# Which engine computes the rests of the rounded weights: from GpSimd to fixed places in the vector engine's order

## What is computed

```python
xn = rms_norm(x, norm_w)
z  = xn @ w_in                                     # 2048 columns in, 8384 out
y_r, S_T = rwkv7_branch(mix(zs), g_r, S0, ...)     # recurrence, gated
o_att    = sum over 3 patterns of dilated_band_attention(q, k, v, ...) * silu(g_a)
y = x + concatenate([y_r, o_att]) @ w_out
```

## Time and profile before

| | |
|---|---|
| median of the 3 runs shown | 1743.68 us (1742.6 to 1744.62) |
| span of the profiled execution, first to last instruction | 1741.7 us |
| what lies around the span, against that median | 2.0 us |
| TensorE busy | 1626.1 us, 93% |
| vector engine (DVE) busy | 814.8 us, 47% |
| ScalarE (ACT) busy | 571.7 us, 33% |
| GpSimd (POOL) busy | 529.7 us, 30% |
| of that the rests, L426, x164 | 397.8 us |

### The profile page before, as it was taken

One profiled execution on the slowest core, in us unless ns is written; L12 is line 12 of the kernel. 1 busy time (PEld: TensorE's weight loads), 2 busy tenths in 40 slices (PEclk: granted clock), 3 DMA queues, 4 the chain that ended last, 5 costly groups with the idle time before them and its releaser, 6 DMA issues.

```text
span 1741.7 us, 32851 instructions
## 1 busy us (share of the span) xinstructions
PE 1626.1 (93%) x12525; PEld 1491.2 (86%) x12525; DVE 814.8 (47%) x1326; ACT 571.7 (33%) x935; POOL 529.7 (30%) x256
## 2 busy tenths in 40 slices
PE   5999989999899998999989999999999999789998
PEld 4988979889798897988979988898888988569998
DVE  3145564655646557465575544263443634420000
ACT  5242232422324223232242333334343343432221
POOL 0333232232322323223142223232232332433432
PEclk9999999999999999999999999999999999899999
DMA  5320220302203022030220544435344363525443
GB/s 185 93 73 18 63 58 3 105 13 62 58 1 103 17 63 58 1 96 25 56 73 26 131 104 121 88 99 139 78 121 98 89 139 78 153 73 146 127 113 87
DMA packets 249819, 140.88 MB, mean 81 GB/s; under 512 B 11053, under 2 KB 242798, under 8 KB 249198
## 3 DMA queue, kind: packets, MB, share of 16 engines
q1 hardware_dynamic: 228156, 126.23, 28.2%
q10 hardware_dynamic: 21570, 13.23, 2.5%
HBM read 124.11 MB, written 15.26 MB: 80 GB/s over the span
## 4 chain that ended last, share of the span: by engine, by line
PE 84%; DVE 7%; issue 4%; ACT 1%; DMA 1%; SPq 1%; POOL 1%; DVEq 0%; ACTq 0%; POOLq 0%
PE acc L442 50%; PE head_banks L858 5%; PE head_banks L882 5%; PE head_banks L1035 2%; PE head_banks L1062 2%; PE head_banks L1017 2%; PE head_banks L894 2%; DVE AREN L1523 2%; PE head_banks L1029 1%; DVE AREN L1585 1%; PE head_banks L792 1%; PE head_banks L759 1%; DVE AREN L1763 1%; PE head_banks L775 1%; PE head_banks L910 1%
## 5 line engine op out<-in xcount | busy, mean ns | idle before, releaser
L426 POOL TENSOR_TENSOR WL<-WR,WH 128x1024 fp32r<-128x1024 f32 (+1 forms) x164 | 397.8, 2426 | 943.4 <-ACT WH L418 935.2
L442 PE MATMUL acc<-XH,WH 128*128 128x260 f32 (+1 forms) x2624 | 595.6, 308 | 20.1 <-POOL XL L692 10.3
L442 PE MATMUL acc<-XL,WH 128*128 128x260 f32 (+1 forms) x2624 | 531.6, 284 | 0.0
L442 PE MATMUL acc<-XH,WL 128*128 128x260 f32 (+1 forms) x2624 | 531.5, 284 | 0.0
L442 PEld LDWEIGHTS acc<-XH,WH 128*128 128x128 f32 (+1 forms) x2624 | 412.0, 191 | 59.6 <-issue 29.3
L442 PEld LDWEIGHTS acc<-XL,WH 128*128 128x128 f32 (+1 forms) x2624 | 408.2, 190 | 0.0
L442 PEld LDWEIGHTS acc<-XH,WL 128*128 128x128 f32 (+1 forms) x2624 | 407.5, 190 | 0.0
L418 ACT ACTIVATE WH<-WR 128x1024 fp32r<-128x1024 f32 (+1 forms) x164 | 171.7, 1047 | 147.0 <-PE acc L442 123.9
L652 POOL TENSOR_TENSOR AREN<-AREN,CA 128x1024 f32<-128x1024 f32 x40 | 87.0, 2176 | 163.6 <-PE head_banks L858 81.3
L1226 ACT ACTIVATE AREN<-head_banks 128x512 f32<-128x512 f32 x80 | 47.9, 599 | 215.2 <-PE head_banks L894 114.1
L858 PE MATMUL head_banks<-AREN 128*128 128x128 f32 x640 | 89.4, 299 | 22.0 <-DVE AREN L1585 19.3
(11 more groups left out here) (234 smaller groups left out, 1939.1 us busy)
## 6 DMA issues: line engine op xcount, KB each, us to landing
WR<-in_w_in SPq DMA_DIRECT2D x128, 512.0 KB, 4.1
WR<-in_w_out SPq DMA_DIRECT2D x32, 512.0 KB, 5.8
out<-AREN ACTq DMA_DIRECT2D x32, 256.0 KB, 2.7
AREN<-in_cache_k_win SPq DMA_DIRECT2D x16, 384.0 KB, 8.5
AREN<-in_cache_v_win SPq DMA_DIRECT2D x16, 384.0 KB, 8.6
mix_scratch<-AREN ACTq DMA_DIRECT2D x16, 260.0 KB, 2.6
AREN<-in_x_prompt SPq DMA_DIRECT2D x4, 1024.0 KB, 7.9
AREN<-in_cache_k_win SPq DMA_DIRECT2D x8, 512.0 KB, 7.3
```

Source lines behind the costliest of these rows:

```text
L426: pool.tensor_tensor(WL[:, k % 2, :, 0:M], WR[:, k % 4, :, 0:M], WH[:, k % 2, :, 0:M].bitcast(F32), ALU.subtract).then_inc(s_lo, 1)
L442: mm = pe.matmul(acc[0:M, hf, 0:HT], w[:, k % 2, j, 0:M], x[:, kt, hf * HT:(hf + 1) * HT], start=(kt == 0 and n == 0), stop=(kt == KT - 1 ...
```

## The change

GpSimd keeps the gate, the five masked products and the slope products; the rests that it formed in the pairs (8 in each of the 8 recurrence pairs, 8 in each of the first 7 attention pairs) go to the vector engine, each at one fixed place of its order. GpSimd still forms those ahead of the first pair and those of the output projection, and the vector engine waits once for the former, GpSimd once for the last of the moved ones.

```diff
-        def rest_half(pool, g, k, M=128):
+        def rest_half(eng, g, k, M=128):
...
-        def pool_feed(pool, span, g, name, ahead=True):
-            for u in span[name]:
-                if u % 8 == 1 and (ahead or u // 8 < 7):
-                    rest_half(pool, g, u // 8 + 1)
...
-                for name in ("lora", "kk", "tail", "bonus", "vec", *GRAMS):
-                    feed(name)
...
-                    if l == 1:
-                        for name in ("tokb", "tokk", "tokv", "nn23", "bcast"):
-                            feed(name)
-                    if l > 1:
-                        for s in ("qt", "dx", "tr"):
-                            for h in "ab":
-                                feed(f"{s}{l - 1}{h}")
-                for name in PE_A.names[PE_A.index[f"qt{last - 1}a"]:]:
-                    feed(name)
...
+            pool.wait_ge(s_lo, 4 * GROUP_C + 1)
             rest_half(pool, GROUP_C, 1)
...
+            dve.wait_ge(s_lo, 4 * group_a(0) + 9)
+
+            def pair_a(i, g, next_shift=True):
...
                    .then_inc(a_dve, DVE_A.one("ssm"))
+                rest_half(dve, g, 1)
...
                    .then_inc(a_dve, DVE_A.one("prod"))
+                rest_half(dve, g, 2)
...
                     for h in range(2):
                         masked(c, h, banks[h])
+                    if c == 2:
+                        rest_half(dve, g, 3)
...
                         dve.tensor_copy(flat(QT[:, 4:8, :]), HB[:, 0, :]).then_inc(a_dve, DVE_A.one(f"qt{l}"))
...
+                    if l in (1, 5):
+                        rest_half(dve, g, 4 + l // 5)
                     for h in range(2):
                         dve.wait_ge(a_pe, PE_A.at(i, f"dx{l}{'ab'[h]}"))
...
                 after("sw")
+                rest_half(dve, g, 6)
                 state(1)
...
                 state(2)
+                rest_half(dve, g, 7)
...
                     shift(i + 1, group_a(i + 1))
+                rest_half(dve, g, 8)
...
                 qs.then_inc(b_dve, DVE_B.one("qs"))
+                rest(1)
...
                 dve.tensor_tensor(GGB, GGB, ZB[:, 3, :], ALU.mult).then_inc(b_dve, DVE_B.one("gate"))
+                rest(2)
...
+                    if t == 1:
+                        rest(3)
...
+                    if j in (0, 2, 5):
+                        rest({0: 4, 2: 5, 5: 6}[j])
                     if j + 2 < nj:
                         largest(j + 2)
...
                    .then_inc(b_dve, DVE_B.one("smx"))
+                rest(7)
...
                 dve.tensor_tensor(MIXB[:, 0:T], HB[:, 3, :], GGB[:, 0:T], ALU.mult).then_inc(b_dve, DVE_B.one("mixp"))
+                rest(8)
```

More of the change, by code:

```diff
@@ L418, in round_half @@
             act.activation(WH[:, k % 2, :, 0:M], WR[:, k % 4, :, 0:M], ACT.Copy).then_inc(s_hi, 1)
-        def rest_half(pool, g, k, M=128):
-            pool.wait_ge(s_w[k % 4], (g + (k // 4 + 1)) * 16)
-            pool.wait_ge(s_hi, g * 4 + (k + 1))
+        def rest_half(eng, g, k, M=128):
+            eng.wait_ge(s_w[k % 4], (g + (k // 4 + 1)) * 16)
+            eng.wait_ge(s_hi, g * 4 + (k + 1))
             if not (isinstance(g, int) and 4 * g + k < 2):
-                pool.wait_ge(s_half, g * 4 + (k - 1))
-            pool.tensor_tensor(WL[:, k % 2, :, 0:M], WR[:, k % 4, :, 0:M],
+                eng.wait_ge(s_half, g * 4 + (k - 1))
+            eng.tensor_tensor(WL[:, k % 2, :, 0:M], WR[:, k % 4, :, 0:M],
                                WH[:, k % 2, :, 0:M].bitcast(F32), ALU.subtract).then_inc(s_lo, 1)
@@ L636, in _, with pair_a @@
                 rest_half(pool, group_a(0), k)
-            def pair_a(i, g, ahead=True):
-                def feed(name):
-                    pool_feed(pool, span_a, g, name, ahead)
+            def pair_a(i):
                 pool.wait_ge(a_act, ACT_A.at(i, "sgg"))
                 pool.tensor_tensor(GG, GG, Z[:, 3, 1:TT + 1], ALU.mult).then_inc(a_pool, POOL_A.one("gate"))
-                for name in ("lora", "kk", "tail", "bonus", "vec", *GRAMS):
-                    feed(name)
                 for l in range(1, last):
@@ L653, in pair_a, with pair_b @@
                         .then_inc(a_pool, POOL_A.one(f"nm{l}"))
-                    if l == 1:
-                        for name in ("tokb", "tokk", "tokv", "nn23", "bcast"):
-                            feed(name)
-                    if l > 1:
-                        for s in ("qt", "dx", "tr"):
-                            for h in "ab":
-                                feed(f"{s}{l - 1}{h}")
-                for name in PE_A.names[PE_A.index[f"qt{last - 1}a"]:]:
-                    feed(name)
[L664 to L673, removed]
+            with pool.Fori(0, PAIRS) as i:
+                pair_a(i)
+            def pair_b(i):
                 pool.wait_ge(b_dve, DVE_B.at(i, "sl"))
@@ L681, in pair_b @@
                     .then_inc(b_pool, POOL_B.one("bts"))
[L682 to L687, removed]
+            with pool.Fori(0, PAIRS) as i:
+                pair_b(i)
+            pool.wait_ge(s_lo, 4 * GROUP_C + 1)
             rest_half(pool, GROUP_C, 1)
@@ L1508, in shift @@
                 mix.then_inc(a_mix, DVE_M.one("mix"))
-            def pair_a(i, next_shift=True):
+            dve.wait_ge(s_lo, 4 * group_a(0) + 9)
+            def pair_a(i, g, next_shift=True):
                 def after(name):
@@ L1676, in _ @@
             with dve.Fori(0, PAIRS - 1) as i:
-                pair_a(i)
-            pair_a(PAIRS - 1, next_shift=False)
+                pair_a(i, group_a(i + 1))
+            pair_a(PAIRS - 1, group_b(0), next_shift=False)
             dve.wait_ge(a_pe, PE_A.start(PAIRS))
@@ L1690, in _, with pair_b, rest @@
             dve.wait_ge(s_zero, 2)
-            def pair_b(i):
+            def pair_b(i, g, fills=True):
+                def rest(k):
+                    if fills:
+                        rest_half(dve, g, k)
                 def after(name):
@@ L1792, in pair_b @@
                 ms.then_inc(b_dve, DVE_B.one("mixs"))
-            with dve.Fori(0, PAIRS) as i:
-                pair_b(i)
+            with dve.Fori(0, PAIRS - 1) as i:
+                pair_b(i, group_b(i + 1))
+            pair_b(PAIRS - 1, 0, fills=False)
             dve.wait_ge(o_mix, done(PAIRS, PAIRS, 16))
```

## The result

The changed kernel takes 1747.17 us (median of 15 runs, 1743.21 to 1751.4), the kernel before 1743.64 us beside it (15 runs, 1740.55 to 1746.15). The ratio is 1.002, with a 95% interval of 1.0012 to 1.0028: slower by 0.2%, 3.5 us. The forecast was 1750.0 us, its own range 1744 to 1756.

A forecast was written before the change was run, and what follows sets the result against it. TensorE, busy 1626.1 of 1741.7 us, was taken as the bound, so only its waits count. Recurrence +8.7 and attention -2.3, about +6.3 us with rounding, on 1743.7 gave 1750.0 us, own range 1744 to 1756, 8 in 10: 1737 to 1765.

The forecast's parts named there:

- wait before `bonus`: Recurrence, L775: scans no longer held by GpSimd's rest 1, so `prod` comes earlier; six pairs -1.0, two -0.4: -6.8 us.
- spells of 1.2 GHz: Recurrence, behind L775: the wait falls to 1.7 us and draws no slow-clock spell; 5 x -1.55 = -7.7 us.
- rest 2: Recurrence, behind `prod`: waits for its rounding but loses a block, ending just before TensorE reaches the grams; cost nothing, cover 0.1 us.
- rest 3, before L780: Recurrence: partly hidden in a 0.70 us idle hole, the remainder reaches TensorE through the fourth chunk's grams; 8 x 0.4 = +3.2 us.
- wait before the first level: Recurrence, L858: `nm2` holds `xtm` or `xt` instead of a rest, `xtb` comes 0.3 us earlier; -2.4 us, spells left there.
- rest 4 behind `nm3`: Recurrence, between `qt1` copy and `xa`: held by GpSimd, it makes TensorE's L894 2.0 us late; +16.0 us, the largest term.
- rest 5: Recurrence, level 5: no `nm` beside it, a 0.2 us gap hides part; some +0.8 us each, +6.4 us.
- `pn`: Attention, first block: no longer slowed beside a GpSimd rest, so TensorE's 0.7 us wait per pair goes; 7 x -0.7 = -4.9 us.
- rest 7, before `pwt`: Attention, behind `smx`: `spm` starts 0.5 us later, 0.3 us of TensorE's time taken; 7 x 0.3 = +2.1 us.
- The faster one: Rival, recurrence: the slightly shorter wait before L858 draws no slow-clock spell; 9 x -1.56 = -14 us, 1736 us; chance 0.20.
- the slower one: Rival, recurrence: the new 2.0 us wait before L894 draws a spell in every pair; +12.5 us, 1762.5 us; chance 0.20.
- rest 4 gets ahead of `nm3`: No-change rival, recurrence: or it is not held by `nm3`, costing 0.8 us; 9.6 us go, 1740.4 us; chance 0.13.

The follow-up runs named there:

- all places: Changed kernel with rests 4 and 5 behind `xb`, `nm2` behind `xtb`, scans to `gl` ahead of `ssm`, rest 3 behind the last masked gram: 1684.39 us, ratio 0.9659.
- two changed orders: Kernel before, all rests on GpSimd, scans to `gl` ahead of `ssm`, rest 4 and `nm2` behind it held until `xtb`: 1692.14 us, ratio 0.9701.
- the one with the scans first: Kernel before, all rests on GpSimd, with the scans and decay steps to `gl` moved ahead of `ssm` on the vector engine: 1718.96 us, ratio 0.986.

## Why the prediction was right

The direction, the mechanism and most terms held; the sum was +6.3 us and +3.4 came out, by the two spans. Term by term, measured from the two profiles:

| term | forecast | measured | from |
|---|---|---|---|
| wait before `bonus` | -6.8 | -4.5 | 18.2 and 1.4 of waits for a rest just before it in pairs 0 and 7, to 15.1 |
| spells of 1.2 GHz | -7.7 | -10.9 | 15 to 8, at 1.55 us |
| rest 2 | 0 | 0 | from L775 to the matmuls of L792 that wait, and from L748 to those of L765, 10.71 us without a spell |
| rest 3, before L780 | +3.2 | +2.7 | 2.0 to 4.7 |
| wait before the first level | -2.4 | -1.7 | 22.0 to 20.3, with pair 7 |
| rest 4 behind `nm3` | +16.0 | +16.7 | below |
| rest 5 | +6.4 | +6.1 | below |
| the loop's edge | none | -1.1 | 10.3 to 9.2 |
| **recurrence** | **+8.7** | **+7.3** | the stretch itself: +7.2 |
| `pn` | -4.9 | -5.5 | 0.92 in each of pairs 1 to 6, below |
| rest 7, before `pwt` | +2.1 | +1.6 | 0.24 in each of pairs 1 to 6, 0.15 in pair 0, start to start |
| late load, pair 0 | +0.5 | +0.2 | the wait 3.99 to 4.52; the step behind it 0.19 later |
| **attention** | **-2.3** | **-3.7** | the stretch itself: -3.8 |

**Rests 4 and 5.** The wait that the profile shows for rest 4, 1.80 us, is less than what it costs. Where nothing is waited for, the transposes (L894) begin 0.15 us before the matmuls ahead of them (L882) end, by the ends that the profile gives, and this overlap is lost too. The cost is read from start to start, in pairs without a spell, first the kernel before (pair 7):

```profile
911.82 2.02 PE L858 MATMUL head_banks<-AREN 128*128 128x128 f32 x16 [2.72 <-issue]
913.68 2.10 PE L882 MATMUL head_banks<-AREN 128*128 128x128 f32 x16
915.63 0.61 PE L894 MATMUL head_banks<-CA,AREN 128*128 128x128 f32 x4
...
917.97 1.95 PE L858 MATMUL head_banks<-AREN 128*128 128x128 f32 x16
```

and the kernel after (pair 4):

```profile
587.13 2.05 PE L831 MATMUL head_banks<-AREN 128*128 128x128 f32 x16 [2.53 <-DVE AREN L1562]
...
595.37 1.95 PE L831 MATMUL head_banks<-AREN 128*128 128x128 f32 x16
```

One level took 6.15 us and takes 8.24, 2.09 more: the forecast was 2.0. Pairs 0 to 2, with a spell in this level in both kernels, give 1.82 to 2.14. The level of rest 5, read in the same way, went from 6.18 to 6.94 us: 0.76, where 0.8 was forecast. The rest itself took 2.52 us and ended 1.08 us after `nm3`, as worked out. The Trainium skill (SBUF — State Buffer, "Who interferes with whom") has the engine that issues first hold the port for its whole instruction, and the row of 2.52 us, behind an `nm3` that began 0.56 us earlier, agrees.

**The attention.** There, too, more goes than the profile's wait. In the attention's pair 2 the step from the first L1017 to the first L1035 (L990 and L1008 after), first before, then after:

```profile
1150.15 0.38 PE L1017 MATMUL head_banks<-AREN 128*128 128x128 f32 x2
...
1156.15 0.43 PE L1035 MATMUL head_banks<-AREN 128*64 128x128 f32 x2
```

```profile
1156.87 0.38 PE L990 MATMUL head_banks<-AREN 128*128 128x128 f32 x2
...
1161.95 0.43 PE L1008 MATMUL head_banks<-AREN 128*64 128x128 f32 x2
```

It went from 6.00 to 5.08 us: 0.92, where the wait for `pn` had been 0.71. The whole pair went from 72.00 to 71.32 us, and each of pairs 1 to 6 did the same within 0.03.

**What was mis-sized.** "6 x -1.0 and 2 x -0.4" for rest 1: only five pairs had the wait of 2.67 us in the trace of before. Pair 6 stood at 1.51 already, and pairs 0 and 7 gained nothing, because a wait for GpSimd's rest of 0.7 us just ahead of `bonus` went into the longer wait at `bonus` itself. That is 2.3 us too much gain. In the other direction, "I leave the spells there" for the wait before the first level: two of its seven spells went, and two double ones became single ones, and the one behind the loop's edge went, against two new ones behind L867 and one behind L748. The count came to -7, not -5, and the gain to 3.2 us more. In the attention "7 x -0.7" had one pair too many, since pair 0 had no such wait, and too little for each, 0.92.

**The rivals.** The faster one (the seven spells behind the first level go) came true in two pairs of seven, the slower one (a new spell behind L894 in each pair) in two of eight: each is a matter of degree. That the sum came near is in part luck: the prediction left the spells behind the first level as they were, and its 2.3 us too much gain at rest 1 and 3.2 too little at the spells nearly cancelled. That rest 4 gets ahead of `nm3` did not happen. The Trainium skill's rule (Perfetto Trace Analysis, "Optimizing Scalar/DVE Operations") that moving work between these two engines might not help fits this change as it stands, 1747.2 us. With all places the move gives 1684.4, and two changed orders with no rest moved give 1692.1: the places decide, and the move is worth some 8 us on top of them.

## What to carry to other kernels

When work moves between the vector engine and GpSimd, look first at which instruction comes next behind the new place, and which GpSimd instruction is released by the same event; the costliest place here was between the copy and the subtraction that TensorE waits for. Try the order before the move: here two changed places in the kernel before gain 3.0%, and the move on top of that 0.4%. Read a new wait from start to start of the same step, since the idle time shown for it was 1.80 us where 2.09 were lost.

## What the runs showed of the hardware

**A one-operand instruction is held too.** The prediction spoke of vector instructions with two operands in SBUF, though its `pn`, 2.29 us beside a rest, is a `TENSOR_SCALAR` with one tensor operand. `t1`, which reads one tensor from SBUF, took 492 ns in the median in the kernel before and 2528 in the one with the scans first, beside GpSimd's rest. Those with an operand in PSUM, `xa` and `xb`, kept 0.69 us beside `nm2` and `nm3`.

**The length of a wait alone does not decide on the clock.** After a wait of 2.51 to 2.54 us at L831 of the changed kernel the clock fell in five pairs and not in pairs 3, 4 and 7; after 1.80 us at L867 it fell in pair 3 and not in pair 4; at L748 it fell after 2.23 us in pair 7 and not after 2.57 in pair 0. What else decides stays open. What a spell costs varies a little: from L748 to the matmuls of L765 that wait it is 12.25 us in pair 7 and 10.71 in pair 6, 1.54 us; in the first doubling level of the changed kernel, 9.57 to 9.88 us with one spell against 8.24 without, it is 1.33 to 1.64.
